# The Sync queue of a mixer-and-experts layer: expert tiles between the mixer's last weight pieces, and the shared odd up tile in two rows

## The reference

```python
xn = rms_norm(h, norm1_g); z = xn @ w_in                    # 1024 x 4096
u, q, k, v, g_ssm, g_att = jnp.split(z, split_at, axis=-1)
y_ssm = s5_branch(u, ...)          # chunked state-space part, GLU with w_glu
y_att = diff_attention(q, k, v, ...)
mixed = sigmoid(g_ssm + b) * (y_ssm @ w_proj_ssm) + sigmoid(g_att + b) * (y_att @ w_proj_att)
h = h + mixed @ w_out
hn = rms_norm(h, norm2_g)
# mixture of experts: 32 experts, 4 of them for each token
logits = hn @ w_router + b_router; top_v, top_i = lax.top_k(logits, 4)
# per expert e and its tokens:
hup = xb @ w_up[e] + b_up[e]       # w_up[e]: 1024 x 2048
act = glu * sigmoid(1.702 * glu) * (lin + 1)
y = act @ w_down[e] + b_down[e]    # w_down[e]: 1024 x 1024
h = h + (weighted sum over the token's experts)
```

## Time and profile before

| | before |
|---|---|
| median of 3 runs | 1146.78 us (1145.4 to 1146.95) |
| span of the profiled execution | 1142.5 us |
| TensorE busy | 1095.7 us, 96% |
| DMA, mean over the span | 381 GB/s, 435.13 MB |
| DMA in the slices from the mixer's end to the last but one | 403 to 430 GB/s |
| granted TensorE clock | 0.9 or more of full speed in every slice |

### The profile page before, as it was taken

The page is one execution under the profiler, slowest core; times in us unless marked ns, Lnnn a source line. Parts: engine busy times, 40 slices in busy tenths (PEclk is TensorE's granted clock), DMA queues, the critical chain, the costliest instruction groups (busy, mean ns, idle before and its releaser), DMA issues.

```text
span 1142.5 us, 14277 instructions
## 1 busy us (share of the span) xinstructions
PE 1095.7 (96%) x5292; PEld 446.9 (39%) x5292; DVE 298.4 (26%) x804; ACT 166.3 (15%) x343; POOL 34.1 (3%) x51
## 2 busy tenths in 40 slices
PE   7999999999999999999999999999999999999997
PEld 4468887633333333333333333333333333333332
DVE  5987244242111111111111111111111111111111
ACT  3043440221111111111111111111111111111110
POOL 6020010000000000000000000000000000000000
PEclk9999999999999999999999999999999999999999
DMA  8734489999999999999999999999999999999996
GB/s 229 200 123 87 140 284 352 366 361 403 427 428 427 429 430 427 429 430 428 428 430 429 427 430 427 428 430 427 428 430 428 427 430 429 427 430 429 427 428 269
DMA packets 63578, 435.13 MB, mean 381 GB/s; under 512 B 19856, under 2 KB 28096, under 8 KB 38592
## 3 DMA queue, kind: packets, MB, share of 16 engines
q1 hardware_dynamic: 57776, 433.17, 92.6%
q0 software_dynamic: 608, 1.34, 0.6%
q10 hardware_dynamic: 5168, 0.27, 0.3%
HBM read 432.01 MB, written 1.57 MB: 380 GB/s over the span
## 4 chain that ended last, share of the span: by engine, by line
PE 58%; DMA 38%; DVE 2%; ACT 1%; issue 1%; SPq 0%; DVEq 0%; ACTq 0%
DMA arena<-in_w_up 38%; PE bank L1066 23%; PE bank L1111 9%; PE bank L635 5%; PE bank L673 4%; PE bank L619 3%; PE bank L1010 2%; PE bank L995 2%; PE bank L949 2%; PE bank L873 1%; PE bank L858 1%; PE bank L846 1%; DMA arena<-in_w_in 1%; PE bank L805 1%; PE bank L937 1%
## 5 line engine op out<-in xcount | busy, mean ns | idle before, releaser
L1066 PE MATMUL bank<-arena 128*64 128x512 f32 x2048 | 452.6, 594 | 30.2 <-DMA arena<-in_w_up 29.9
L1066 PEld LDWEIGHTS bank<-arena 128*64 128x64 f32 x2048 | 143.7, 137 | 331.8 <-issue 271.5
L1111 PE MATMUL bank<-arena 128*64 128x512 f32 x1024 | 226.8, 595 | 0.0
L1809 DVE TENSOR_SCALAR arena<-bank 128x256 f32<-128x256 f32 x64 | 27.2, 425 | 499.1 <-PE bank L1066 499.1
L1111 PEld LDWEIGHTS bank<-arena 128*64 128x64 f32 x1024 | 70.7, 137 | 133.9 <-issue 133.1
L1367 ACT ACTIVATE arena<-arena 128x256 f32<-128x256 f32 x64 | 26.6, 417 | 451.7 <-DVE arena L1810 451.7
L619 PEld LDWEIGHTS bank<-arena 128*128 128x128 f32 (+1 forms) x450 | 49.2, 143 | 89.6 <-issue 82.1
L619 PE MATMUL bank<-arena 128*128 128x128 f32 (+1 forms) x450 | 75.2, 290 | 8.9 <-DMA arena<-in_x 5.1
L1010 PE MATMUL bank<-arena 64*128 64x512 f32 x256 | 63.9, 616 | 0.7 <-ACT arena L1375 0.7
L995 PE MATMUL bank<-arena 128*64 128x512 f32 x248 | 60.1, 605 | 0.0
L1774 DVE TENSOR_SCALAR arena<-arena 128x128 f32 (+3 forms) x126 | 33.3, 327 | 92.7 <-issue 92.6
(11 more groups left out here) (294 smaller groups left out, 517.0 us busy)
## 6 DMA issues: line engine op xcount, KB each, us to landing
arena<-in_w_up SPq DMA_DIRECT2D x125, 2048.0 KB, 25.5
arena<-in_w_down SPq DMA_DIRECT2D x63, 2048.0 KB, 26.8
arena<-in_w_in SPq DMA_DIRECT2D x16, 1024.0 KB, 6.0
arena<-in_w_up SPq DMA_DIRECT2D x5, 1024.0 KB, 6.4
arena<-in_w_out SPq DMA_DIRECT2D x4, 1024.0 KB, 7.8
arena<-in_w_proj_ssm SPq DMA_DIRECT2D x8, 256.0 KB, 5.8
arena<-in_w_proj_att SPq DMA_DIRECT2D x2, 1024.0 KB, 7.9
arena<-in_w_down SPq DMA_DIRECT2D x2, 1024.0 KB, 31.6
```

The source lines that it names most:

```text
L1066: last = pe.matmul(B[n][64 * h:64 * h + 64, :], xg[:, 2 * j + r, :], rows[r][2 * h + n], start=False, stop=(j == order[-1] and r == 1), sk ...
L1111: last = pe.matmul(B[3][64 * n:64 * n + 64, :], (actT_last if last_block else actT)[:, k % 4, k // 4, :], dn_w[parity][k // 4][:, k % 4, 5 ...
L1809: TS(part(glu_t, n), v[:, 0], LIMIT, None, ALU.min)
```

## The change

The loop over the pieces now ends with piece 15. Behind it the queue's program is written out. Each of the pieces 16 to 20 has one expert tile ahead of it or behind it, and the first of the tiles is issued as soon as `y_ps` is 2, ahead of piece 16. The two down tiles of block 0 stand behind pieces 19 and 20, where they stood behind piece 23. Piece 24 stands ahead of piece 19. The shared odd up tile of block 1 is loaded in two rows (halves of 1024 KB), one at `mixed`, one at `out_ps` 5; the loads of `b_up` stand ahead of the down tiles of block 1. In block 1, the refill of that shared up tile for block 3 is issued when TensorE has read it, ahead of two other refills; before, it stood behind them.

```diff
-            for i in (*range(21), PIECES - 1, *range(21, PIECES - 1)):
+            for i in range(16):
...
+            def load_piece(i):
+                sp.wait_ge(piece_used, 16 if i == PIECES - 1 else i - RING + 1)
+                for dst, src in piece(i):
+                    sp.dma_start(dst, src).then_inc(last_in if i == PIECES - 1 else slot_in[i % RING], 16)
...
+            sp.wait_ge(s["y_ps"], 2)
+            load_up_tile(0, 0, 0, 0)
+            load_piece(16)
+            load_up_tile(0, 0, 0, 1)
+            load_piece(17)
+            load_up_tile(0, 0, 0, 2)
+            load_piece(18)
+            load_up_tile(0, 0, 0, 3)
+            load_piece(PIECES - 1)
+            load_piece(19)
+            sp.wait_ge(s["yT_ps"], 2)
+            load_dn(0, 0, 0, 1)
+            load_piece(20)
+            load_dn(0, 0, 0, 0)
+            load_piece(21)
+            sp.wait_ge(s["oT"], 1)
+            load_up_tile(1, 1, 1, SHARED + 1)
+            load_piece(22)
+            load_piece(23)
             sp.wait_ge(s["mixed"], 4)
+            load_row(up_w[1][SHARED][:, 0], 1, 0, SHARED).then_inc(s["ahead_in"], 16)
             load_ahead_part(3)
+            for q in range(4):
+                sp.dma_start(bup[E * q:E * q + E], b_up[:, 512 * q:512 * q + 512]).then_inc(bup_in, 16)
             load_dn(1, 1, 1, 0)
             sp.wait_ge(s["out_ps"], 3)
-            for q in range(4):
-                sp.dma_start(bup[E * q:E * q + E], b_up[:, 512 * q:512 * q + 512]).then_inc(bup_in, 16)
             load_dn(1, 1, 1, 1)
             sp.wait_ge(s["out_ps"], 5)
-            load_up_tile(1, 1, 1, SHARED)
+            load_row(up_w[1][SHARED][:, 1], 1, 1, SHARED).then_inc(up_in[1][SHARED], 16)
             load_ahead_part(2)
...
             load_downs(2, 2, 0)
+            sp.wait_ge(s["up_used"], UT + ORDER.index(SHARED) + 1)
+            load_up_tile(3, 3, 1, SHARED)
             sp.wait_ge(s["up_used"], UT + ORDER.index(0) + 1)
             load_row(up_w[0][0][:, 0], 2, 0).then_inc(up_in[0][0], 16)
             sp.wait_ge(s["up_used"], UT + ORDER.index(1) + 1)
             load_up_tile(2, 2, 0, 1)
-            load_ahead(3, 3, 1)
+            sp.wait_ge(s["up_used"], 2 * UT)
+            load_up_tile(3, 3, 1, SHARED + 1)
             load_downs(3, 3, 1)
```

More of the change, by code:

```diff
@@ L340, in _ @@
               .then_inc(s["a_in"], 16)
-            ups_after = {17: (0,), 18: (1,), 19: (2,), 23: (3,)}
-            downs_after = {23: (1, 0)}
-            for i in (*range(21), PIECES - 1, *range(21, PIECES - 1)):
+            for i in range(16):
                 if i == 12:
@@ L353, in _ @@
                                 .then_inc(s["m_in"], 16)
-                if i == PIECES - 1:
-                    sp.wait_ge(piece_used, 16)
-                elif i >= RING:
+                if i >= RING:
                     sp.wait_ge(piece_used, i - RING + 1)
-                arrived = last_in if i == PIECES - 1 else slot_in[i % RING]
+                arrived = slot_in[i % RING]
                 if i > 0:
@@ L391, in _, with load_row @@
                               .then_inc(s["vec_in"], 16)
[L392 to L405, removed]
+            def load_piece(i):
+                sp.wait_ge(piece_used, 16 if i == PIECES - 1 else i - RING + 1)
+                for dst, src in piece(i):
+                    sp.dma_start(dst, src).then_inc(last_in if i == PIECES - 1 else slot_in[i % RING], 16)
+            def load_row(dst, e, r, j=0):
+                return sp.dma_start(dst, w_up[e, 2 * P * j:2 * P * (j + 1), :]
+                                    .rearrange("(p r) (h n) -> r p h n", r=2, h=2)[r])
             def load_ahead_part(q):
@@ L1045, in expert_block @@
                     elif j < SHARED:
-                        if ahead and j == 0:
-                            pe.wait_ge(s["ahead_in"], 80)
-                        else:
+                        if not (ahead and j == 0):
                             pe.wait_ge(up_in[parity][j], 16 * b + 16)
                     else:
+                        if ahead and j == SHARED:
+                            pe.wait_ge(s["ahead_in"], 16 * 6)
                         pe.wait_ge(up_in[parity][j], 8 * b + (8 if parity else 16))
```

## The result

The changed kernel takes 1156.64 us (median of 6 runs, 1154.66 to 1161.48) against 1146.62 us of the kernel before on the same chip: 0.98% slower, ratio 1.0098 (95% interval 1.0087 to 1.011). The forecast was slower, by 2.7 us; it is 10.0 us, outside the range.

A forecast was written before the change was run, and what follows sets the result against it. The prediction took TensorE's time up to about 284 us, plus the stream's lag and constants, as the bound. A 3.5 us stall on piece 22 less 0.8 us won gave +2.7 us, 1149.5 us, range 1145.5 to 1151.0 us.

The forecast's parts named there:

- 9.3 us x 0.97 = 9.0 us: Before piece 22: idle queue time at 133.5 to 138.4 and 142.8 to 147.2 us recovered, against 14.7 us of extra data.
- 6.9 for a tile alone: On the queue: a tile with nothing else in flight lands 6.9 us after its issue at the earliest.
- Piece 20 in time by 1.2 us: Line 858: piece 20 lands at 184.9 us, wanted at 186.1, so no stall there.
- piece 21 in time by 0.5 us: Start of the out-projection: piece 21 lands at 192.5 us, wanted at 193.04, so no stall there.
- 0.8 us won: Block 0's refills: moving the half tile to `mixed` lets the stream start earlier; 0.8 us taken, between 0 and 2.4.
- The whole 2.4 us: Block 3's first down tile: the stream's lag there, the most any queue order could win from there on.
- The working's 218 GB/s: Pieces 17 and 18: rate assumed for their 32-partition parts, from 4.9 us a piece.
- No stall: Rival, 26%: pieces don't wait for tiles issued ahead, or their lag shrinks; only 0.8 us won remain, 1146.0 us.
- Faster: Rival, 6%: no stall, and the whole 2.4 us lag at block 3 is won, 1144.4 us.
- The longer stall: Rival, 8%: piece 20, 21 or 23 is late too, 4.5 us or more lost, 1151 us.
- The rule on 358 GB/s: Skill's HBM-side limit: a tile takes 5.9 us, three 17.6 us, stall 6.4 us; the prediction said the trace disagrees.

The follow-up runs named there:

- p128: The changed kernel with pieces 16 to 18 each loaded by one DMA over 128 partitions instead of four over 32: 1148.6 us, ratio 1.0016.
- p128_two: p128 with one down tile of block 0 moved back behind piece 23: 1146.2 us, ratio 0.9994.
- late_only: The kernel before with only the change's later edits (shared up tile in two rows, b_up loads, block 1 refill): 1145.9 us, ratio 0.9997.
- mixer_only: The changed kernel with its later edits undone, so only the order around the mixer's pieces is new: 1154.6 us, ratio 1.0083.
- mixer_again: mixer_only run a second time, beside fill22 on the same chip: 1157.6 us, ratio 1.0094.
- tile_ahead: early_only with up tiles 1 and 2 issued right ahead of pieces 17 and 18, not right behind 16 and 17: 1146.8 us, ratio 1.0003.
- fill22: mixer_only with 6 matmuls whose results are not needed ahead of TensorE's wait for piece 22: 1156.8 us.
- late19: The kernel before with piece 19 held back until the attention output stands, piece 20 directly behind, no extra bytes: 1153.1 us, ratio 1.006.
- filled: The changed kernel with unneeded matmuls ahead of TensorE's waits, 8 for piece 19 and 6 for piece 22: 1152.8 us, ratio 1.0059.
- light_tail: The kernel before with half of each of block 3's two down tiles not loaded, 2 MB less: 1145.6 us, ratio 0.9995.
- early_only: mixer_only without the three extra tiles ahead; the first tile still goes out early, at y_ps 2: 1146.8 us, ratio 1.0006.
- rev_parts: early_only with the four parts of pieces 16 to 18 issued in the opposite order: 1147.0 us, ratio 1.0013.
- late19_filled: late19 with 8 unneeded matmuls ahead of TensorE's wait for piece 19: 1156.3 us, ratio 1.01.

## Why the prediction was wrong

**What held.** The end stands at TensorE's time up to block 3, and what delays block 0 delays the end: out_ps 1 was 10.1 us later than the 202.7 us of an unstalled run whose clock started as late, and the timed median is 10.0 us up. A piece that lands late stalls TensorE, piece 22 is the one that decides, and a tile ahead of it is worth 4.9 us (p128 against p128_two). Refills and the half tile changed nothing. Slower was right.

**The step that failed: "9.3 us x 0.97 = 9.0 us" of idle time recovered.** Measured from the issue of piece 15, piece 22 landed 10.7 us later than before in place of 5.7: 14.7 - 10.7 = 4.0 us recovered. (By late_only, which has the order of before up to there, it is 9.8 us later and 4.9 recovered.) In mixer_only it was 7.7, in mixer_again 3.1. That step carries 5 us of the miss, and it varies from run to run by nearly as much.

The bytes moved show where the 9.0 us went. These are three stretches of before and the same three of the changed kernel, 2.4 us later, in which TensorE does the same work up to the first stall; then the middle one of mixer_only, 2.6 us later. The last number of a row is GB/s:

```profile
133.50:147.20 13.70, 13.70 (x75) 12.28 (x75) 3.50 (x13) 7.73 (x19) 0.00 (x0) 1.00 0.34 79
147.20:168.00 20.80, 20.21 (x91) 16.02 (x90) 10.10 (x28) 11.69 (x26) 1.25 (x3) 1.00 1.01 319
168.00:191.00 23.00, 23.00 (x109) 20.24 (x108) 14.13 (x14) 1.06 (x1) 2.71 (x4) 1.00 1.02 373
```

```profile
135.90:149.60 13.70, 13.70 (x75) 12.28 (x75) 3.50 (x13) 7.72 (x19) 0.00 (x0) 1.00 0.97 313
149.60:170.40 20.80, 20.23 (x91) 16.04 (x90) 10.11 (x28) 11.67 (x26) 1.26 (x3) 1.00 1.04 275
170.40:193.40 23.00, 19.89 (x78) 16.69 (x78) 11.38 (x10) 1.06 (x1) 2.68 (x4) 0.85 1.03 382
```

```profile
149.80:170.60 20.80, 20.23 (x91) 16.03 (x90) 10.12 (x28) 11.66 (x26) 1.28 (x3) 1.00 1.04 313
```

In the first stretch 3.2 MB more were moved, which is 7.5 us at 428 GB/s, and not 9.0. (The first tile, issued into an idle queue at 134.66 us, landed 9.9 us later, where the working had 6.9 for a tile alone; here the parts of piece 16 followed it.) In the second, pieces 16 to 18 with the tiles between them moved at 275 GB/s, where it was 319: 2.1 us lost again. The third gives 0.5 us back. That makes 5.9 us in the mean of the engines. Piece 22 has landed only when the last of its data is in, and that was 4.0. I had taken the idle stretches at full rate, and the three pieces of 32 partitions at the 4.9 us each that they had before. The same second stretch ran at 313 GB/s in mixer_only, with the same queue: that is about half of the 3.7 us between the two.

Neither p128 nor tile_ahead proves what slows this stretch. p128 recovers 10.9 us, but frees some 7 us of the queue by its shape alone; tile_ahead's landing of piece 18 is within the spread of the others.

**What was missing: the price of the clock.** I costed a stall at its length. Behind its waits the changed kernel had 6.8 and 3.4 us at half clock. Where the clock stays, out_ps 1 stands 3.8 us after piece 22's landing (fill22, p128, late19, filled); with 3.4 us at half clock behind it, 5.2 to 5.5; with 6.8 us, 6.8. So 1.5 to 3.0 us on top, 1.7 here. The Trainium skill, "TensorE: Matmul & The Clock Gate", section "HAM oscillation — how this bites in real kernels", works the loss out as throttled time times (1 - 1.2/2.4), that is half of it; 3.1 of 6.8 and 1.7 of 3.4 us agree. The waits behind which the clock fell were 2.2 and 3.1 us long in the changed kernel, and 2.7 to 4.6 us in others; behind waits of 1.4 and 1.7 us (late19, p128) it stayed.

The sum then is closed. Piece 22 at 207.4 and 5.4 us to out_ps 1 is 212.8; less 202.7 is 10.1 us. The first stall and its 3.3 us at half clock are not in it: TensorE would have had to wait for piece 22 anyway. (Its issue at 194.93 us waited for TensorE too, but the tile ahead of it on the queue landed only at 204.7 us, so that cost nothing.) In order of size, 8.4 us are piece 22's lateness (207.4 against a want at 199.0), 1.7 are the clock. Against the forecast's +2.7 us that is 4.9 us more of stall, 1.7 us of clock and 0.8 us that were not won.

**Neighbours.** "Piece 20 in time by 1.2 us" and "piece 21 in time by 0.5 us" were wrong, by the same step: they landed at 192.2 and 199.8 us, where an unstalled TensorE would have wanted them at 188.6 and 195.6. It didn't wait for them only because it had already stalled. Piece 19, which I didn't list, was 3.1 us late and the first to stall, though in the end it cost nothing of its own. Before, it landed 7.3 us ahead of its want; newly ahead of it were a tile and piece 24, 7.3 us of data.

**"0.8 us won".** Nothing was. The down tile of 283.96 does land sooner after its issue with an emptier queue (7.8 us in the changed kernel for 9.3), as the working said. But I had looked one step too early for the transfer that the stream starts from: block 3's first up tile, issued 10.3 us later, takes 9.5 us with either. light_tail won 1.1 us at that tile with 2 MB taken out, and 0.6 us in the median, which is within its interval. The whole 2.4 us were not there to be had. (The working's 218 GB/s is 214 by its own 4.9 us a piece, which changes nothing.)

**The rivals.** No stall was wrong (early_only and p128_two show that state: 1146.8 and 1146.2). Faster was wrong. The longer stall, to which I gave 8%, was the case, and 1151 us was too little for it. Of the chances, piece 20 and 21 had margins of 1.2 and 0.5 us against a term of 9.0 that I had measured in no row; that was the place to widen the range. The rule on 358 GB/s (the Trainium skill, "DMA: Bandwidth & Descriptors", section "Where 436 GB/s comes from"), which came out at 6.4 us of stall, is nearer to the result, and still not its cause: the stream runs at 426 GB/s from 310 to 455 us.

**What stays open.** Why the last quarter of pieces 16 to 18 is late with the tiles where the change puts them, and whether the order of the parts or their partitions have to do with it. Which engine moves what isn't told apart in these views. The changed kernel itself was not run with its tiles issued as in tile_ahead, so what that would save isn't known. And why the same queue landed piece 22 up to 5 us apart was not looked into.

## What to carry to other kernels

Before you fill a queue's idle time, find what waits behind the filler: a weight that is wanted at a set time pays for every byte ahead of it, and an idle stretch is worth less than its length if the transfers around it don't run at full rate when they overlap. Look for the last late arrival ahead of the point that sets the end (here the start of block 0); stalls before it are covered by it, and filling them saves nothing. Price a stall of TensorE of some 3 us at its length plus half of the stretch at half clock behind it. And where the bound follows TensorE, loading ahead wins nothing, whatever the DMA idles.

## What was not expected of the hardware

- Four DMAs of 256 KB over 32 partitions each, among tiles on the same queue: the last quarter of piece 18 came 2.7 to 6.2 us after the third in the eight profiles with the changed order, 0.9 us in tile_ahead and 1.0 us in late_only. With all engines busy the stretch of these pieces moved 275 to 319 GB/s, and 426 to 431 later.
- The clock at the start: full speed from 8.5 to 8.9 us in three of the sixteen profiled executions (before, rev_parts, late19_filled) and from 12.9 to 14.3 us in the others, worth 2.4 us between the two main profiles, ahead of anything that the change touches.
- The same queue (mixer_only, mixer_again) had piece 22 at 203.9 and at 209.0 us, while piece 15 was issued at 125.0 and 125.6 us.
